# Experts in two lanes of 64 slots, with the weights as TensorE's stationary operand

## What is computed

```python
gate = softmax(top2 of the router's logits in the token's best group) * p_group
expert_id = group * 8 + top2 index            # 4 groups of 8 experts, 2 experts for each token
h = silu(xblk @ w1[e]) * (xblk @ w3[e])       # w1, w3: 1024 x 512 for each of 32 experts
y = h @ w2[e]                                 # w2: 512 x 1024
out[token] += gate * y
```

## Time and profile before

| | |
|---|---|
| Median of 3 runs | 2130.78 us (2127.84 to 2132.82) |
| Profiled execution | 2130.82 us, of which the span is 2129.0 us |
| Granted TensorE clock, mean | 0.947 |
| PE matmuls busy | 1782.7 us (84%) |
| PE weight loads busy | 1022.7 us (48%) |
| DVE busy | 1496.2 us (70%) |
| ACT busy | 1039.1 us (49%) |
| DMA | 417.62 MB, mean 196 GB/s |

### The profile page before, as it was taken

One profiled execution on the slowest core, in us unless ns is written; L12 is line 12 of the kernel. 1 busy time (PEld: TensorE's weight loads), 2 busy tenths in 40 slices (PEclk: granted clock), 3 DMA queues, 4 the chain that ended last, 5 costly groups with the idle time before them and its releaser, 6 DMA issues. The chain is left out here.

```text
span 2129.0 us, 41055 instructions
## 1 busy us (share of the span) xinstructions
PE 1782.7 (84%) x11690; PEld 1022.7 (48%) x11693; DVE 1496.2 (70%) x1855; ACT 1039.1 (49%) x1362; POOL 553.7 (26%) x456
## 2 busy tenths in 40 slices
PE   3488989799389996999914999999999889899947
PEld 0366666344177774555512454544444444444412
DVE  2576666488689996888978345666769888755537
ACT  2234243677378886333204134445556666534326
POOL 0000000000057785333313121223324323222213
PEclk9799999999799998999956999999999999999979
DMA  9321220565563322344336357886979999887537
GB/s 377 90 90 60 89 79 36 200 220 180 181 228 119 116 90 90 119 158 141 136 109 236 112 155 216 289 295 205 364 242 374 374 377 372 295 276 222 181 82 274
DMA packets 167790, 417.62 MB, mean 196 GB/s; under 512 B 16233, under 2 KB 24881, under 8 KB 166065
## 3 DMA queue, kind: packets, MB, share of 16 engines
q1 hardware_dynamic: 152898, 362.85, 46.8%
q0 software_dynamic: 14832, 54.01, 10.4%
HBM read 343.38 MB, written 73.44 MB: 196 GB/s over the span
## 5 line engine op out<-in xcount | busy, mean ns | idle before, releaser
L2060 DVE SCALAR_TENSOR_TENSOR arena<-arena 128x2048 f32 (+1 forms) x186 | 421.3, 2289 | 108.1 <-ACT arena L2004 50.9
L2140 PE MATMUL ps<-arena 128*128 x1200 | 458.3, 382 | 44.0 <-DVE arena L2060 43.8
L2141 PE MATMUL ps<-arena 128*128 x1200 | 458.1, 382 | 0.0
L2142 PE MATMUL ps<-arena 128*128 x1200 | 457.9, 382 | 0.0
L1998 ACT ACTIVATE arena<-arena 128x2048 f32 (+1 forms) x124 | 233.2, 1908 | 149.5 <-DMA arena<-w 62.3
L640 PE MATMUL ps<-arena 128*128 128x256 f16 (+1 forms) x1680 | 235.1, 301 | 21.1 <-DVE arena L525 21.1
L2140 PEld LDWEIGHTS ps<-arena 128*128 128x128 f16 x1200 | 118.0, 98 | 185.3 <-issue 59.0
L640 PEld LDWEIGHTS ps<-arena 128*128 128x128 f16 x1680 | 164.7, 99 | 85.7 <-DVE arena L525 15.2
L2142 PEld LDWEIGHTS ps<-arena 128*128 128x128 f16 x1200 | 118.1, 98 | 139.8 <-issue 3.4
L2141 PEld LDWEIGHTS ps<-arena 128*128 128x128 f16 x1200 | 117.9, 98 | 131.6 <-issue 3.5
L2004 ACT ACTIVATE arena<-arena 128x2048 f32 (+1 forms) x62 | 117.4, 1908 | 69.1 <-DMA arena<-w 52.6
(11 more groups left out here) (296 smaller groups left out, 3272.8 us busy)
## 6 DMA issues: line engine op xcount, KB each, us to landing
arena<-w SPq DMA_DIRECT2D x186, 1024.0 KB, 12.1
arena<-hT_d SPq DMA_DIRECT2D x64, 512.0 KB, 6.0
arena<-w_mod SPq DMA_DIRECT2D x16, 1536.0 KB, 8.0
h_d<-arena SPq DMA_DIRECT2D x17, 512.0 KB, 3.0
x_d<-arena SPq DMA_DIRECT2D x17, 512.0 KB, 2.6
arena<-x SPq DMA_DIRECT2D x8, 1024.0 KB, 6.4
hT_d<-arena SPq DMA_DIRECT2D x16, 512.0 KB, 3.1
arena<-x SPq DMA_DIRECT2D x16, 512.0 KB, 4.8
```

Source lines behind the costliest of these rows:

```text
L2060: return nc.vector.scalar_tensor_tensor(dst, src, scale, high, ALU.mult, ALU.subtract)
L2140: pe.matmul(out, high, part(buf, whi, at, 512), start=first, stop=False)
L2141: pe.matmul(out, high, part(buf, wlo, at, 512), start=False, stop=False)
L2142: return pe.matmul(out, low, part(buf, whi, at, 512), start=False, stop=last)
```

## The change

Slots are rounded up to units of 64 for each expert. The row of units is cut in two lanes at `steps` = the larger of half the units and the largest group's units. Step n works on unit n in lane 0 and on unit `steps` + n in lane 1; the two lanes' rows are gathered together as one tile of 128 rows. With the counts above there are 40 steps; lane 0 starts 11 experts and lane 1 starts 21. 4 steps start an expert in both lanes (steps 0, 11, 13, 21), 24 in one lane (1, 3, 5, 6, 8, 9, 12, 14 to 19, 22, 26, 27, 30 to 32, 34 to 38), and 12 in none.

- In `product` the weights (128 by 128) are stationary and a lane's 64 columns of rows move. The hidden rows come out transposed already, so `transposes_h` goes; the result of `down` comes out transposed, so ACT copies it to `yT` (`keep_y`) and PE transposes it (`transposes_y`, 8 transposes in f32), two steps late.
- Each lane has one set of split weights and not two. The staging area has 8 slots: 2 for w1 in each lane, and 2 each for w3 and w2, which both lanes share.
- There is one `x` buffer and not two. Waits on `dn_mm`, `y_tr` and `yT_ev` are new.
- `phase_route` makes other tables: a word for each step that holds both lanes' start flags and counts, made by four small matmuls and scans in place of comparisons over all pairs of block and expert. It loads 8 pieces and not 6 at its end.

```diff
@@ phase_route
-            link(V.tensor_scalar(b["nbi"].bitcast(I32), b["nbi"].bitcast(I32), 7, None, ALU.arith_shift_right))
+            link(V.tensor_scalar(b["nbi"].bitcast(I32), b["nbi"].bitcast(I32), 6, None, ALU.arith_shift_right))
...
-            count_le(one(b["ebf"]), 64, b["rend"])
...
+            for r in range(2):
+                link(V.tensor_tensor_scan(one(b[f"run{r}"]), one(b["one72"]), rows[r], 0.0, ALU.mult, ALU.add))
...
-            for n in range(N13 + N2):
-                load_piece(sp, g, first, n)
+            for e, kind, lane in ((e0, 0, 0), (e1, 0, 1), (e0, 1, 0), (e0, 2, 0)):
+                for p in range(PER):
+                    load_piece(sp, g, e, kind, lane, p)
@@ phase_experts, SP
+            second = table(sp, TAB_E1, 0, NE - 1)
+            weights(second, 1, 1, 1)
+            for_step(1, (0, 1))
+            weights(second, 2, 1, 1)
+            for_step(2, (0, 1))
+            with sp.Fori(2, steps) as n:
+                for_step(n - 1, (2,))
+                for_step(n + 1, (0, 1))
@@ ACT
+            def step(n):
+                if at_least(n, 2):
+                    keep_y(n - 2)
+                    down_weights(n - 1)
...
+                with act.If(fresh[0] == 1):
+                    act.wait_ge(up1_mm, START + 2 * n + 1)
+                    split(0, 0, own[0])
+                silu(n)
+                with act.If(fresh[1] == 1):
+                    split(0, 1, own[1])
+                with act.If(fresh[0] == 1):
+                    act.wait_ge(up3_mm, START + 2 * n + 1)
+                    split(1, 0, both[0])
+                x_high(n + 1)
+                with act.If(fresh[1] == 1):
+                    split(1, 1, both[1])
+                h_high(n)
@@ DVE
+            def step(n):
+                if at_least(n, 2):
+                    down_weights(n - 1)
...
+                fresh, own, both = starts(dve, n + 1)
+                with dve.If(fresh[0] == 1):
+                    split(0, 0, own[0])
+                if at_least(n, 2):
+                    scale_y(n - 2)
+                with dve.If(fresh[1] == 1):
+                    split(0, 1, own[1])
+                with dve.If(fresh[0] == 1):
+                    split(1, 0, both[0])
+                hidden(n)
+                x_low(n + 1)
+                with dve.If(fresh[1] == 1):
+                    split(1, 1, both[1])
+                h_low(n)
@@ PE
-            def product(out, high, low, buf, at, first, last):
-                pe.matmul(out, high, part(buf, whi, at, 512), start=first, stop=False)
-                pe.matmul(out, high, part(buf, wlo, at, 512), start=False, stop=False)
-                return pe.matmul(out, low, part(buf, whi, at, 512), start=False, stop=last)
+            def product(out, lane, at, moving, first, last):
+                high, low = moving
+                pe.matmul(out, whi[lane][:, at:at + P], high, start=first, stop=False)
+                pe.matmul(out, whi[lane][:, at:at + P], low, start=False, stop=False)
+                return pe.matmul(out, wlo[lane][:, at:at + P], high, start=False, stop=last)
...
+            def up(kind):
+                for lane in range(2):
+                    for f in range(KE):
+                        out = ps[:, kind, f * P + lane * UNIT:f * P + (lane + 1) * UNIT]
+                        for k in range(KD):
+                            mm = product(out, lane, kind * KD * D_EXP + k * D_EXP + f * P, halves(xh, xl, k, lane), k == 0, k == KD - 1)
+                    mm.then_inc((up1_mm, up3_mm)[kind], 1)
...
+            def step(n):
+                up1(n)
+                if at_least(n, 2):
+                    transposes_y(n - 2)
+                up3(n)
+                transposes_x(n + 1)
+                if at_least(n, 1):
+                    down(n - 1)
```

More of the change, by code:

```diff
@@ L1747, in _ @@
[L1747 to L1751, removed]
+            link(V.tensor_tensor_scan(b["pend"], b["one32"], b["nb"], 0.0, ALU.mult, ALU.add))
@@ L1935, in _, with weights @@
[L1935 to L1939 removed]
+            steps = step_count(sp, 0)
+            def weights(e, kind, lane, turn):
+                done, base = of_lane(lo, kind, lane)
+                for p in range(PER):
+                    sp.wait_ge(done, base + PER * turn + p - 1)
+                    sp.sem_inc(g["alone"], 1)
+                    load_piece(sp, g, e, kind, lane, p)
@@ new lines, in h_high, with keep_y, down_weights @@
+                nc.scalar.activation(hh, b["h"], ACT.Copy).then_inc(h_hi, 1)
+            def keep_y(n):
+                act.wait_ge(dn_mm, START + 2 * n + 2)
+                act.wait_ge(y_tr, n)
+                nc.scalar.activation(b["yT"], ps_row[:, 2048:3072], ACT.Copy).then_inc(yT_ev, 1)
+            def down_weights(n):
+                fresh, own, both = starts(act, n)
+                for lane in range(2):
+                    with act.If(fresh[lane] == 1):
+                        act.wait_ge(dn_mm, START + 2 * n)
+                        split(2, lane, both[lane])
@@ L2054, in _ @@
+            for lane in range(2):
+                split(0, lane, 0)
+            split(1, 0, 0)
+            x_high(0)
+            split(1, 1, 1)
+            step(0)
+            step(1)
+            with act.Fori(2, steps) as n:
+                step(n)
+            keep_y(step_count(act, 2))
+            last = step_count(act, 1)
+            down_weights(last)
+            keep_y(last)
         @block.vector
         def _(dve):
-            nb = blocks(dve)
+            steps = step_count(dve, 0)
@@ L2117, in _ @@
+            split(1, 0, 0)
             x_low(0)
-            split2(0, 0)
-            split13(1, 1, 0, N13)
-            hidden(0)
-            x_low(1)
-            step(1, 0)
-            with dve.Fori(2, nb) as n:
-                step(n, n - 1)
-            last = dve.value_load(tab[0:1, TAB_NB1:TAB_NB1 + 1], min_val=31, max_val=MAX_BLOCKS - 2)
-            h_low(last)
+            split(1, 1, 1)
+            step(0)
+            step(1)
+            with dve.Fori(2, steps) as n:
+                step(n)
@@ L2127, in _ @@
+            last = step_count(dve, 1)
+            down_weights(last)
+            scale_y(step_count(dve, 2))
             scale_y(last)
@@ L2197, in combine_ln2 @@
 def combine_ln2(arena):
-    return arena_slices(arena, 46000, [("l2g", D), ("l2b", D)])
+    rows = expert_memory(arena)
+    return {name: rows[name] for name in ("l2g", "l2b")}
 def phase_combine(nc, env):
```

486 lines of the change are left out of this document (237 added, 249 removed).

## The result

| | before | after |
|---|---|---|
| Median of 4 runs | 2131.8 us | 2103.11 us (2098.37 to 2105.5) |
| Profiled execution, its span | 2130.82, 2129.0 us | 2105.5, 2103.7 us |
| Granted TensorE clock, mean | 0.947 | 0.919 |
| From the first to the last matmul of the experts | 896 us | 867.6 us |

The ratio is 0.9868, with a 95% interval of 0.9849 to 0.9886: **28.7 us faster, where 72 were forecast**. The direction and PE's own work were right; the stalls were priced too low.

The account below looks back on a forecast made before the run. PE was taken to bound most of the expert phase, weight loads its middle. The terms 743 + 19 + 45 + 12 + 5 = 824 us against 896 gave 72 us less: 2130.8 - 72 = 2059 us, range 2005 to 2140.

Parts of the forecast that it names:

- PE's work: Expert phase: 40 steps of 18.6 us, 743 us against 843 before, 100 us less for PE.
- doubles: Steps 11, 13 and 21, where both lanes start an expert: 15 us each, 45 in all, between 0 and 25 each.
- steps with one start: The 24 steps that start one expert: 1.2 us charged for 16 of them, 19 us.
- start: First two steps of the expert phase: 12 us more than 2 x 18.6, between 0 and 20.
- end: End of the expert phase: `down`, `keep_y`, 8 transposes and `scale_y` follow each other, 5 us more than before.
- PE's rate: Expert matmuls, each with its own weight load: 29.2 ns each, 16.8 us for the 576 of a step.
- rival of the slow long stream: Expert matmuls in a long stream run slower than the burst: deciding from 32.3 ns, 2990 us at 69.5 ns; chance 0.13.
- The jump back: End of PE's loop: between 0 and 1.15 us a jump, 0 to 44 us in 38 jumps; taken as 0.
- single weights expose the loads: Expert phase: weights come 3.8 us late in each of 27 steps, 2162 us; chance 0.11.
- The route phase: Phase ahead of the experts: ends 13 us behind `placed` and not 18.8, 5 us less, paying for the later start.
- The third rival: Expert phase: the doubles' wait is made up in steps without loads, 20 of 45 us stay, 2015 us; chance 0.16.
- 30 or more around 11, 13 and 21: Sign in the expert phase: x's transposes 30 us or more apart around steps 11, 13 and 21.

Follow-up runs that it names:

- after, again: The changed kernel, unchanged, run again on another chip as the measure for three others: 2111.16 us.
- half of DVE's splits: Against the changed kernel, DVE makes the low part of only half of each weight piece and PE reads that half twice: 2076.63 us.
- half loads: Against the changed kernel, half of each weight piece is loaded; ACT and DVE read it twice and still write whole pieces: 2059.87 us.
- no singles: Against the changed kernel, lane 1's new experts in steps 14, 16 and 18 are left out: 2096.07 us.
- own slots: Two runs against the changed kernel, each with two more staging slots for lane 1: for w3 2098.43 us, for w2 2097.28 us.

## Why the prediction was wrong, and where it was right

The forecast's sum was 743 + 19 + 45 + 12 + 5 = 824 us from first to last matmul. By T0 to T40 after's 867.6 come apart as follows. The undisturbed work is 60.6 us from the first matmul to T4 (four steps' `up`s, two `down`s, five groups of transposes), 36 steps of 18.67, and 13.9 behind T40 (two `down`s, three groups of transposes), 746.6 in all.

| term | forecast | measured |
|---|---|---|
| PE's work | 743 | 746.6 |
| doubles | 45 | 68.3 |
| steps with one start | 19 | 14.3, of which 8.2 at T19 |
| start | 12 | 30.3 |
| end | 5 | 8.1 |

The sum is 43.6 us above the forecast's. The doubles have 23.3 of that and the start 18.3.

- **PE's rate, right.** 29.2 ns over whole steps, at a granted clock of 1.00. The burst of 15 in the earlier trace rows gave the price, and the rival of the slow long stream is out. The Trainium skill ("TensorE: Matmul & The Clock Gate", back-to-back issue gap) has about 81 ns for sustained pairs with 128 columns; no run here shows that form, and at 64 columns a pair takes little more than a third of it.
- **The jump back, right at 0.** Every undisturbed distance has one jump in it, between the last matmul of `down` and the first of `up`. In after these two start 0.08 us apart and not 0.03, which is 2 us in 38 jumps. In after, again, three of the later distances (from T26, T27 and T31) have 0.34 to 0.36 us there. The Trainium skill ("Runtime: NRT & Kernel Launch", instruction fetch mechanics) has an engine wait for a fetch behind a taken branch outside the fetched pages; nothing near the 1.15 us of the earlier trace rows is seen at this jump.
- **Steps with one start, right within 5 us, but in other places.** The forecast charged 1.2 us for 16 of them, though it names 12, because DMA needs 19.6 us a step. Measured are 2.0 us from T12 to T18 and 4.1 from T34 on. DMA's lag was probably made up while PE stood in the doubles (argued from the windows, not tried). The 4.1 us (T34 and T36) are not DMA's: with half of DVE's splits they are gone, with half loads 3.3 stay. In addition came 8.2 us at T19, where lane 0 starts right behind lane 1, which the prediction did not see. There it is the loads: half loads and no singles each take 6.4 of it, half splits 0.8. The rival "single weights expose the loads" is out for single starts: it asked for 3.8 us each, and leaving three out saved 7 us.
- **The doubles, the mechanism right and the size not.** The prediction named them, with the shared staging and `x_low` behind the splits, and charged 15 us each, 25 at most. They cost 68.3 / 3 = 22.8; without them the kernel is 69 us faster, and with the same starts moved apart 71 us. **The step of the prediction that failed is this price.** It has two parts, DVE's work (31.4 us less a step of 18.6 is 12.8) and one late load (w2 of lane 1, 6 to 12 us), and 15 us is little more than either alone, as if they ran side by side. The runs show more than that: a load starts only when DVE has split the slot's old piece, ACT copies only when it has landed, and DVE splits only behind ACT, and this comes for w3 as for w2 (own slots take 17.1 and 22.3 us off). Halving both load and split takes 39.5 us off, either alone 11 to 14. Part of the price is the clock: in the five distances 570 matmuls stand about 53 ns apart in place of 29, 13.6 of the 68.3 us. How the rest divides between a bare chain and links that take turns stays open, and so do the 31 us that are left with both halved.
- **The start, the term that was mis-sized most.** 30.3 us for 12, two and a half times the price. The prediction saw that lane 1's w3 and w2 are asked for only when lane 0's are split, and charged 12 us without a working. The rows show waits of 2.37, 2.38 and 8.96 us for splits in the first two steps, 8.3 us in three waits behind them, and a PEclk of 0.89 from 1158 to 1249: 252 matmuls stand about 54 ns apart, 6.1 us. Half loads take 14.3 of it and half splits 7.0: here the chain load, copy, split is bare.
- **The clock, not in the sum.** After the longer pauses the matmuls are nearly twice as far apart (last section). In the double of step 13 PEclk was 0.76 over 49 us. The prediction had no term for it, though the earlier trace rows showed 0.83 at before's start; its 13.6 and 6.1 us stand in the doubles and the start above.
- **The route phase, right in its sum.** Behind `placed` the phase ends 13.8 us later and not 18.8, and from there the first matmul comes after 18.9 us and not 14.8: -5.0 and +4.1, where -5 and +4.6 were forecast. Another 1.1 us came ahead of `placed`, where no change was forecast. The first matmul of the experts came 5.8 us later than before's in the profiled executions; 5.6 of that were there already some 20 us ahead of `placed`, and after, again had its first matmul 2.6 us sooner, so this lies between executions.

The third rival, stalls that overlap, is out too: the doubles cost more than was charged, not less. Of the signs that the prediction named, "30 or more around 11, 13 and 21" held in kind (30.2, 46.0, 28.4), and five distances and not three were long; T23, for which 18.6 was named, is one of them (29.5).

## What to carry to other kernels

Count coincidences, not loads. An average over the phase (650 us of DMA for 743 of PE) hid that three steps with two starts cost 68 us and the steps with one cost 14. Where the buffers of a pipeline hold one set, price a doubled step by its whole chain from free slot to split piece, and add what PE's slower clock costs after its pauses. A schedule that spreads the same starts over neighbouring steps takes 66 us out of the five distances here, where half loads and half splits together take 39.5. A kernel that does so and still computes the layer was not built.

## What the runs showed of the hardware

- A weight load of 128 by 128 in f16 and a matmul of 64 columns issue every 29.2 ns for whole steps, though the record of one load has 100 ns and that of one matmul 196.
- After the longer pauses of PE in the expert phase the granted clock is down at 1.2 GHz and the distance nearly doubles. Behind the wait of 13.77 us (timeline of PE, after) the matmuls stand 49 to 55 ns apart, at a granted clock of 0.50 from 1444 to 1447, and 28 to 30 ns from 1447.1 on, when it is 1.00 again. It does not follow each wait: behind those of 2.37 and 2.38 us at the start the distances are 29 ns. Three of the slow ones:

```profile
1444.26 0.24 PE L2199 MATMUL ps<-arena 128*128 128x64 f16 x1
1444.31 0.24 PE L2200 MATMUL ps<-arena 128*128 128x64 f16 x1
1444.37 0.24 PE L2198 MATMUL ps<-arena 128*128 128x64 f16 x1
```

- On two of the chips most free steps have one to three pauses of 0.2 to 0.4 us, the larger part of them inside `down`, some at the jump back or at the end of `up`, which no record explains. On the one where after was run again they and small stalls make it 8 us slower, and before by less than 2 (2131.8 and 2133.38 us). The cause stays open.
- DVE's operations on two elements took 3.96 us each while POOL worked on 2304 (route phase of after):

```profile
1125.40 0.15 DVE L1797 TENSOR_SCALAR arena<-arena 128x1 f32<-128x1 f32 x1
...
1125.51 4.03 POOL L1889 TENSOR_TENSOR arena<-arena 128x2304 f16<-128x2304 f16 x1 [15.23 <-DVE arena L1792]
1125.59 3.96 DVE L1798 TENSOR_TENSOR arena<-arena 128x2 f32<-128x2 f32 x1
1129.49 4.03 POOL L1890 TENSOR_TENSOR arena<-arena 128x2304 f16<-128x2304 f16 x1
1129.58 3.95 DVE L1799 TENSOR_TENSOR arena<-arena 128x2 f32<-128x2 f32 x1
```

An operation of the same size took 0.16 us once POOL was done. The Trainium skill ("SBUF — State Buffer", "SBUF: two separate sides") says that a VectorE operation with two SBUF inputs and a GpSimd operation that reads SBUF lock their shared ports against each other for a whole instruction; these rows agree, each DVE operation lasting as long as POOL's beside it. It cost about 1 us here by my estimate: PE waited 6.73 us for DVE's line 1802, which came 0.5 us behind POOL's end, and the matmuls that read POOL's result came another 0.5 us later.
